# Two MLPs without their norm stage: x is transposed as it is, and the squared factor multiplies the MLP's sums

## The chip, the core and the metric

The kernel runs on one core of a Trainium2 chip. The metric is the device time of one execution, in microseconds (us). TensorE multiplies, VectorE and ScalarE evict and prepare, GpSimd (POOL) does little, and SyncE issues the loads of the weights. SBUF holds the data, and PSUM, in eight banks of 128 x 512 fp32, takes TensorE's results.

## The reference

Three blocks run on x (256 tokens by 1024). The change touches the two MLPs, one at the end of each of the first two layers:

```
def rmsnorm(x, g):
    xf = x.astype(jnp.float32)
    y = xf * lax.rsqrt(jnp.mean(xf * xf, axis=-1, keepdims=True) + EPS)
    return (y * g.astype(jnp.float32)).astype(x.dtype)

        x = x + jnp.concatenate([y_tok, y_mem], axis=-1) @ w_out[layer]
        hm = rmsnorm(x, mlp_norm[layer])
        x = x + jnp.square(jax.nn.relu(hm @ w_up[layer])) @ w_down[layer]
```

The factor r of a token, rsqrt(mean + EPS), is positive, and relu and the square let it through: square(relu(r a)) = r^2 square(relu(a)). So r^2 = 1 / (mean + EPS) may as well multiply the token's row of the MLP's result. The rest (a short convolution, attentions, RWKV, SSD, a router with 32 experts) is as before.

## The kernel before, in words

The program is a row of stages, each a block (`meeting`) at whose end all engines meet; only then does the next stage's work start. x lies in SBUF as two tiles of 128 tokens (`x[:, t, :]`). fp32 products are made in three parts: each operand is split into hi (rounded) and lo (the rest), and hi x hi, hi x lo and lo x hi are added up. ScalarE makes each hi part and VectorE each lo part from it.

Around an MLP stand three stages:

- **The output projection** (`add_projection`, a `split_stage` named out0 or out1). Two units of 1024 x 512 weights, each in two halves of four chunks (L449 to L468). The first half of a unit makes 24 products, the second 24. Jobs 0 and 1 are the two token tiles of x's first 512 columns, jobs 2 and 3 of its last 512; job j uses bank j. VectorE adds each full bank to x (L1203), in the order in which `programme` queues it: the split of piece 3 (L513), the additions of jobs 0 and 1, then `split_next` (L535), which splits the MLP's first unit early, then the additions of jobs 2 and 3. ScalarE has the hi parts of the same early split (L502).
- **The norm** (`norm`, L857). TensorE runs 11 warming products (L307). ScalarE and VectorE make the square sums of one token tile each (L871, L887), POOL the factor (L918, L920), both engines a scaled copy of x (L874, L892), TensorE 16 transposes (L910, L913) into eight banks, and ScalarE and VectorE evict each bank with the gain as hi (L879) and lo (L901) into `mlp_h`.
- **The MLP** (`mlp`, L1261). It first zeroes the four sums in banks 4 to 7 (L1304). A loop of four trips with two units each follows. Of a unit, the up products make four groups of 128 columns in banks 0 to 3. Each group takes eight steps k of two products, hi (L1315, 512 moving columns: hi and lo of h) and lo (L1313, L1318, 256). Sums are taken by ScalarE and VectorE two groups at a time: a copy (L1355), an addition (L1388), relu and square (L1391), hi (L1358) and lo (L1394) of the hidden part. 48 down products of three parts (L136 to L138) add into the four sums. Weights for the next unit are split meanwhile (L1349, L1381). At the end the sums are closed by a zero product each (L1255) and added to x (L1412).

Of the kernel before, what the change touches and what calls it, by code (L numbers as in the profile page):

```python
# [32 lines left out]
P = 128  # L33
S = 256
# [98 lines left out]
def three(pe, dst, left, right, start, stop):  # L133

    inside = not (start or stop)
    pe.matmul(dst, left[0], right[0], start=start, stop=False, skip_group_check=inside)  # L136
    pe.matmul(dst, left[0], right[1], start=False, stop=False, skip_group_check=inside)  # L137
    return pe.matmul(dst, left[1], right[0], start=False, stop=stop, skip_group_check=inside)  # L138


# [44 lines left out]
def program(nc, a, out, at, dumps=()):  # L185

    with ExitStack() as ctx:
# [167 lines left out]
        def split_stage(name, units, consume, src, pair=None, depth=3, on_vector=lambda j: j % 2 == 0, loads=(),  # L355
                        act_then=None, dve_then=None, on_pool=None, early=None, ahead=0, warm_after=0):

# [25 lines left out]
            with ExitStack() as on:  # L383
# [21 lines left out]

                def programme(split_w, split_h, empty, later=None, split_next=None):

# [23 lines left out]
                with meeting() as block:  # L431
# [6 lines left out]
                    def _(pe):  # L438
                        keep_warm(pe, 8)
                        for n, (u, first_chunk, products) in enumerate(units):  # L440
                            for half in range(2):
# [25 lines left out]
                                if half == 0 or not products[-1][6]:  # L467
                                    mm.then_inc(used, 1)  # L468
                        if warm_after:
                            quiet = max(0, n_full - n_banks)  # L470
                            pe.wait_ge(free_v if on_vector(quiet) else free_a, nth(quiet))
                            keep_warm(pe, warm_after, quiet % n_banks)

                    @block.scalar
                    def _(act):
# [27 lines left out]

                        programme(split_w, split_h, empty, split_next=split_next)

                    @block.vector
                    def _(dve):
# [28 lines left out]

                        programme(split_w, split_h, empty, later if dve_then else None, split_next)

# [654 lines left out]
        def mlp_first(layer, on):  # L1193

            u = unit[f"mlp{layer}"]
            w = [sb(f"mlp{layer}_w0_" + s, [P, 2, KD // 2, UC], F32R, on=on, side="right") for s in ("hi", "lo")]
            return w, lambda j: stream.view(u)[:, j * KD // 2:(j + 1) * KD // 2, :], u

        def add_projection(name, u0, src, early=None):
# [5 lines left out]
            split_stage(name, token_products(u0, 2), consume, src, on_vector=lambda j: True, depth=2, early=early)  # L1205

# [53 lines left out]

        def mlp(layer, h_both, w_first):  # L1261

# [14 lines left out]
            with ExitStack() as on:  # L1277
# [3 lines left out]
                hid = [sb("mlp_hid_" + part, [P, nm, S], F32R, on=on) for part in ("hi", "lo")]  # L1281
                rec = sb("mlp_rec", [P, nm, S], on=on)
                acc = lambda t, h: ps[:, 4 + 2 * t + h]

# [13 lines left out]
                with meeting() as block:  # L1298
                    @block.tensor
                    def _(pe):  # L1300
                        nought = c_("noughts").bitcast(BF16)
                        for t in range(NT):
                            for h in range(2):
                                pe.matmul(acc(t, h), nought[:, 0:P], nought[:, 0:UC], start=True, stop=False)  # L1304
                        with pe.Fori(0, trips) as i:
                            for b in range(body):
                                w = [[piece_slot(p, b * pieces + half) for p in w_split] for half in range(2)]
                                pe.wait_ge(w_lo, i * (body * pieces) + (b * pieces + 2))
                                for m in range(nm):
                                    for k in range(KD):  # L1310
                                        hi, lo = (p[:, k % 4, m * P:(m + 1) * P] for p in w[k // 4])
                                        if k:
                                            pe.matmul(ps[:, m, 0:S], lo, h_both[:, k, 0:S], start=False, stop=False,  # L1313
                                                      skip_group_check=True)
                                        mm = pe.matmul(ps[:, m], hi, h_both[:, k, :], start=(k == 0),  # L1315
                                                       stop=(k == KD - 1), skip_group_check=True)
                                        if not k:
                                            pe.matmul(ps[:, m, 0:S], lo, h_both[:, k, 0:S], start=False, stop=False,  # L1318
                                                      skip_group_check=True)
                                    if m % 2:  # L1320
                                        mm.then_inc(ups, 1)
                                for half in range(2):
                                    j = b * pieces + 2 + half
                                    w = [piece_slot(p, j) for p in w_split]
                                    pe.wait_ge(w_lo, i * (body * pieces) + (j + 1))

                                    pe.wait_ge(hid_lo, i * (body * nb) + (b * nb + half + 1))
                                    for k in range(2):
                                        f = 2 * half + k
                                        for t in range(NT):  # L1330
                                            for h in range(2):
                                                mm = three(pe, acc(t, h), [p[:, f, t * P:(t + 1) * P] for p in hid],
                                                           [p[:, k, h * UC:(h + 1) * UC] for p in w],
                                                           start=False, stop=False)
                                    mm.then_inc(downs, 1)
                        close_sums(pe, closed)

                    @block.scalar
                    def _(act):
# [25 lines left out]

                        act.activation(begun[:, 0:1], c_("noughts")[0:1, 0:1], ACT.Copy).then_inc(w_hi, 2)
                        for j in range(2, SPLIT):
                            split(0, j)
                        with act.Fori(0, trips - 1) as i:
                            for b in range(body):  # L1370
# [5 lines left out]
                    def _(dve):  # L1376
# [22 lines left out]

                        dve.tensor_copy(begun[:, 1:2], c_("noughts")[0:1, 0:1]).then_inc(w_lo, 2)  # L1400
                        for j in range(2, SPLIT):
                            split(0, j)
                        with dve.Fori(0, trips - 1) as i:
                            for b in range(body):
                                turn(i, b)
                        for b in range(body):
                            turn(trips - 1, b, last=b == body - 1)
                        for t in range(NT):
# [19 lines left out]
        def conv_layer(kn, first):  # L1428
            with ExitStack() as on:
# [72 lines left out]
                attention("mem_attn0", [memory_item(0, t, qT, nconv, [(1, 2, 4)]) for t in range(NT)], cat)  # L1502
                early = mlp_first(0, first)
                add_projection("out0", unit["out0"], cat, early)
                return early[0]

# [302 lines left out]
        def nsa_layer(sh, first, keys, held):  # L1809
            with ExitStack() as on:  # L1810
# [54 lines left out]
                inner.close()  # L1865
                early = mlp_first(1, first)
                add_projection("out1", unit["out1"], cat, early)
                return early[0]

# [1572 lines left out]

        def block_mlp(layer, w_first):
            with ExitStack() as on:
                h_both = sb("mlp_h", [P, KD, 2 * S], F32R, on=on)
# [95 lines left out]
```

## Time and profile before

| | us |
|---|---|
| median of 3 runs (1837.08 to 1841.11) | 1839.04 |
| span of the profiled execution | 1837.7 |
| TensorE busy in it | 1691.4 (92%) |
| VectorE busy | 921.0 (50%) |
| ScalarE busy | 601.6 (33%) |
| POOL busy | 34.3 (2%) |

Busy shares are means over stages with different limits. How long an engine's operations last says nothing of whether they are waited for; that is read in the timeline, from what stands idle before them and what released it. "PEq" as a releaser is a stage border or TensorE's queue. PEclk is the clock granted to TensorE: 1.00 is 2.4 GHz and 0.50 is 1.2 GHz. A product's record is longer than its distance to the next, since products are pipelined.

### The profile page before, as it was taken

How to read it: one execution, taken by the hardware profiler on the slowest of the kernel's cores; microseconds unless marked ns; L12 is line 12 of the kernel's file. 1: busy time of each engine (PE TensorE's matmuls, PEld its weight loads, DVE VectorE, ACT ScalarE, POOL GpSimd, SP SyncE). 2: the span in 40 equal slices, each digit the busy share in tenths (PEclk: the TensorE clock that was granted, in tenths of full speed). 3: DMA queues.
4: the chain of work that ended last, by engine and by line, in shares of the span. 5: the costliest groups of instructions: out<-in, count | busy, mean ns of one | idle time of the engine just before them, and what ended most of it. 6: DMA issues, size and time to landing. Idle time of an engine off the chain costs nothing. (4 is left out here: it accounts for less than half of the span.)

```text
span 1837.7 us, 31324 instructions
## 1 busy us (share of the span) xinstructions
PE 1691.4 (92%) x13407; PEld 1204.0 (66%) x13431; DVE 921.0 (50%) x1471; ACT 601.6 (33%) x875; POOL 34.3 (2%) x53
## 2 busy tenths in 40 slices
PE   7988999898789999998889999979979999999995
PEld 4976888665568887988887895557744444444442
DVE  2576555424865555787765775645642222121112
ACT  1534444213744444332003664534331111111110
POOL 2000000000000000010000000000000000000000
PEclk9999999998999999998999999989999999999998
DMA  8244454242074453420002541443579999999993
GB/s 316 93 183 183 183 183 160 92 147 92 7 269 183 183 183 114 168 88 14 4 4 93 184 145 63 160 166 110 205 301 429 427 426 428 427 427 427 427 427 150
DMA packets 101897, 379.91 MB, mean 207 GB/s; under 512 B 9980, under 2 KB 20463, under 8 KB 89227
## 3 DMA queue, kind: packets, MB, share of 16 engines
q1 hardware_dynamic: 101216, 377.89, 53.0%
q8 instruction: 98, 1.61, 0.4%
q14 instruction: 28, 0.23, 0.0%
q0 software_dynamic: 352, 0.15, 0.0%
q10 hardware_dynamic: 203, 0.04, 0.0%
HBM read 376.92 MB, written 1.14 MB: 206 GB/s over the span
## 5 line engine op out<-in xcount | busy, mean ns | idle before, releaser
L1315 PE MATMUL ps<-mlp_h,mlp_w_hi 128*128 128x512 f32 x512 | 179.1, 398 | 0.0
L3167 PE MATMUL ps<-weight_slots,moe_h 128*64 128x512 f32 x528 | 155.2, 594 | 6.8 <-DMA weight_slots<-in_w_exp_up 3.1
L1381 DVE TENSOR_TENSOR mlp_w_lo<-weight_slots,mlp_w_hi 128x2048 fp32r<-128x2048 f32 x60 | 134.9, 2290 | 45.6 <-ACT mlp_w_hi L1349 45.6
L3167 PE MATMUL ps<-moe_slots,moe_h 128*64 128x512 f32 x496 | 148.1, 593 | 4.0 <-DMA moe_slots<-in_w_exp_up 3.9
L3247 DVE TENSOR_TENSOR moe_hidT<-moe_silu,ps 128x256 f32<-128x256 f32 x32 | 13.5, 421 | 237.3 <-ACT moe_silu L3204 237.3
L1313 PE MATMUL ps<-mlp_h,mlp_w_lo 128*128 128x256 f32 x448 | 126.7, 283 | 0.0
L1349 ACT ACTIVATE mlp_w_hi<-weight_slots 128x2048 fp32r<-128x2048 f32 x60 | 111.4, 1904 | 43.0 <-PE ps L138 43.0
L3167 PEld LDWEIGHTS ps<-weight_slots,moe_h 128*64 128x64 f32 x528 | 50.4, 137 | 106.1 <-issue 105.3
L1315 PEld LDWEIGHTS ps<-mlp_h,mlp_w_hi 128*128 128x128 f32 x512 | 94.1, 190 | 17.5 <-issue 0.3
L136 PE MATMUL ps<-mlp_w_hi,mlp_hid_hi 128*128 128x512 f32 x256 | 101.3, 396 | 0.0
L138 PE MATMUL ps<-mlp_w_hi,mlp_hid_lo 128*128 128x512 f32 x256 | 101.2, 395 | 0.0
L137 PE MATMUL ps<-mlp_w_lo,mlp_hid_hi 128*128 128x512 f32 x256 | 101.2, 395 | 0.0
L307 PE MATMUL ps<-const 128*128 128x512 bf16 x309 | 77.7, 402 | 24.5 <-PEq L217 23.2
L1313 PEld LDWEIGHTS ps<-mlp_h,mlp_w_lo 128*128 128x128 f32 x448 | 85.9, 192 | 2.9
L3202 ACT ACTIVATE moe_grown<-ps 128x512 f32<-128x512 f32 x32 | 19.2, 599 | 209.4 <-PE ps L3167 209.4
L3167 PEld LDWEIGHTS ps<-moe_slots,moe_h 128*64 128x64 f32 x496 | 48.2, 137 | 49.2 <-issue 49.2
L3254 DVE SCALAR_TENSOR_TENSOR moe_y_lo<-ps,moe_slot_gate,moe_y_hi 128x512 fp32r<-128x512 f32 x32 | 24.0, 751 | 112.1 <-ACT moe_y_hi L3207 112.1
L3184 PE MATMUL ps<-moe_slots,moe_hidT 128*64 128x512 f32 x336 | 76.7, 598 | 1.0 <-DVE moe_hidT L3247 1.0
L307 PEld LDWEIGHTS ps<-const 128*128 128x128 bf16 x330 | 31.6, 102 | 63.9 <-issue 34.1
L3207 ACT ACTIVATE moe_y_hi<-ps,moe_slot_gate 128x512 fp32r<-128x512 f32 x32 | 22.0, 687 | 152.1 <-PE ps L3184 152.1
L2686 PE MATMUL ps<-weight_slots,hT 128*128 128x512 f32 x128 | 64.1, 624 | 0.0
L574 PE MATMUL ps<-weight_slots,hT 128*128 128x512 f32 (+2 forms) x160 | 58.6, 526 | 2.5 <-PEq L217 1.9
(641 smaller groups left out, 3944.9 us busy)
## 6 DMA issues: line engine op xcount, KB each, us to landing
weight_slots<-in_w_exp_gate SPq DMA_DIRECT2D x22, 2048.0 KB, 23.2
moe_slots<-in_w_exp_up SPq DMA_DIRECT2D x21, 2048.0 KB, 28.3
moe_slots<-in_w_exp_down SPq DMA_DIRECT2D x21, 2048.0 KB, 26.7
weight_slots<-in_w_in SPq DMA_DIRECT2D x20, 2048.0 KB, 7.9
weight_slots<-in_w_up SPq DMA_DIRECT2D x16, 2048.0 KB, 7.7
weight_slots<-in_w_down SPq DMA_DIRECT2D x16, 2048.0 KB, 7.6
weight_slots<-in_w_exp_up SPq DMA_DIRECT2D x11, 2048.0 KB, 27.2
weight_slots<-in_w_exp_down SPq DMA_DIRECT2D x11, 2048.0 KB, 25.7
```

The source lines that it names most:

```text
L136: pe.matmul(dst, left[0], right[0], start=start, stop=False, skip_group_check=inside)
L137: pe.matmul(dst, left[0], right[1], start=False, stop=False, skip_group_check=inside)
L138: return pe.matmul(dst, left[1], right[0], start=False, stop=stop, skip_group_check=inside)
L307: pe.matmul(ps[:, bank], nought[:, 0:P], nought[:, 0:UC], start=True, stop=True)
L574: mm = pe.matmul(dst, h[:, k, t * P:(t + 1) * P], w[:, k, c0:c0 + width], start=(first and k == 0), stop=(last and k == kc - 1))
L1313: pe.matmul(ps[:, m, 0:S], lo, h_both[:, k, 0:S], start=False, stop=False, skip_group_check=True)
L1315: mm = pe.matmul(ps[:, m], hi, h_both[:, k, :], start=(k == 0), stop=(k == KD - 1), skip_group_check=True)
L1349: act.activation(piece_slot(w_split[0], jj), raw_piece(jj), ACT.Copy).then_inc(w_hi, 1)
L1381: dve.tensor_tensor(piece_slot(w_split[1], jj), raw_piece(jj), piece_slot(w_split[0], jj).bitcast(F32), ALU.subtract).then_inc(w_lo, 1)
L2686: mm = pe.matmul(z_bank(g, t), hT[:, k, t * P:(t + 1) * P], w[:, k, :], start=(k == 0), stop=(k == KD - 1))
L3167: mm = pe.matmul(ps[side(kind), 0, :], h_sel[:, k, :], w[kind][:, k, :], start=(k == 0), stop=(k == KD - 1))
L3184: mm = pe.matmul(ps[side(h), 3, :], hid_T[:, f, :], w_down[:, f, h * UC:(h + 1) * UC], start=(f == 0), stop=(f == nm - 1))
```

## The change

There is no norm stage ahead of an MLP. x itself is transposed and multiplied by the gain alone. Its first 512 columns (`h_near`) are turned inside the last unit of the projection, between its halves: TensorE waits for x's first two additions and makes eight transposes into banks 4 to 7; ScalarE evicts hi and VectorE lo, both queued behind `split_next`. The last 512 columns (`h_far`) are turned at the start of the MLP stage. The up products of each unit now take two column groups together, near halves of both first, then far halves. The first trip is written out ahead of the loop, since in it TensorE waits for `h_far` and since its first down products open the sums, for which the zeroing products go. ScalarE makes the square sums in the MLP stage, behind its first two splits; VectorE makes the factor, and multiplies with it in the last additions.

```diff
+class Turning:
+    def tensor(self, pe, x_ready=None):
+        if x_ready is not None:
+            pe.wait_ge(x_ready, NT)
+        for c in range(KD // 2):
+            for t in range(NT):
+                mm = pe.transpose(self.bank(c)[:, t * P:(t + 1) * P], self.x(t, c), self.ident)
+            mm.then_inc(self.turned, 1)
+    def scalar(self, act):
+        for c in range(KD // 2):
+            act.wait_ge(self.turned, c + 1)
+            act.activation(self.part[:, c, 0:S], self.bank(c), ACT.Copy, scale=self.gain(c)).then_inc(self.led, 1)
+    def vector(self, dve):
+        for c in range(KD // 2):
+            dve.wait_ge(self.led, c + 1)
+            dve.scalar_tensor_tensor(self.part[:, c, S:], self.bank(c), self.gain(c),
+                                     self.part[:, c, 0:S].bitcast(F32), ALU.mult, ALU.subtract).then_inc(self.left, 1)
...
@@ split_stage: programme @@
                         if early and n == len(units) - 1:
                             split_next()
+                        if turn and n == len(units) - 1:
+                            turn()
                         for j in whole[0][n]:
                             empty(j)
@@ split_stage: tensor @@
+                                if turning and half == 0 and n == len(units) - 1:
+                                    turning.tensor(pe, free_v)
...
@@ mlp: tensor @@
-                        nought = c_("noughts").bitcast(BF16)
-                        for t in range(NT):
-                            for h in range(2):
-                                pe.matmul(acc(t, h), nought[:, 0:P], nought[:, 0:UC], start=True, stop=False)
-                        with pe.Fori(0, trips) as i:
+                        def unit_products(i, b, first=False):
...
+                            for m0 in range(0, nm, 2):
+                                for m, k in [(m0 + m, 4 * half + k) for half in range(2) for m in range(2)
+                                             for k in range(4)]:
+                                    if first and k == 4 and m == 0:
+                                        pe.wait_ge(turning.left, KD // 2)
...
+                                            mm = three(pe, acc(t, h), [p[:, f, t * P:(t + 1) * P] for p in hid],
+                                                       [p[:, k, h * UC:(h + 1) * UC] for p in w],
+                                                       start=first and f == 0, stop=False)
...
+                        turning.tensor(pe)
+                        for b in range(body):
+                            unit_products(0, b, first=b == 0)
+                        with pe.Fori(1, trips) as i:
                             for b in range(body):
+                                unit_products(i, b)
@@ mlp: scalar @@
+                        turning.scalar(act)
                         for j in range(2, SPLIT):
                             split(0, j)
+                        for t in range(NT):
+                            act.activation(squares[:, t, :], x[:, t, :], ACT.Square, scale=D ** -0.5,
+                                           accum_out=scale[:, 0, t:t + 1]).then_inc(summed, 1)
@@ mlp: vector @@
+                        turning.vector(dve)
                         for j in range(2, SPLIT):
                             split(0, j)
+                        dve.wait_ge(summed, NT)
+                        dve.tensor_scalar(scale[:, 0, :], scale[:, 0, :], EPS, None, ALU.add).then_inc(added, 1)
+                        dve.wait_ge(added, 1)
+                        dve.reciprocal(scale[:, 1, :], scale[:, 0, :]).then_inc(scale_made, 1)
...
-                                dve.tensor_tensor(part, part, acc(t, h), ALU.add)
+                                dve.scalar_tensor_tensor(part, acc(t, h), scale[:, 1, t:t + 1], part, ALU.mult, ALU.add)
@@ block_mlp @@
-                norm(f"mlp{layer}_norm", x, [("mlp_norm", layer * KD, [h_both[:, :, 0:S], h_both[:, :, S:]])])
-                mlp(layer, h_both, w_first)
+                mlp(layer, h_near, sb("mlp_h_far", [P, KD // 2, 2 * S], F32R, on=on), w_first)
```

## Rows read from the trace of the kernel before

**Rows 1.** Windows: from:to, length, busy us (instructions) by engine, PEclk, DMA share.

```profile
157.19:167.57 10.38, 5.33 (x31) 3.18 (x32) 6.17 (x14) 6.40 (x13) 0.95 (x2) 0.96 0.03 11
528.22:538.22 10.00, 4.96 (x31) 3.08 (x32) 6.17 (x14) 6.03 (x13) 0.94 (x2) 1.00 0.03 13
167.57:171.78 4.21, 4.21 (x19) 3.62 (x17) 3.25 (x2) 2.74 (x2) 0.00 (x0) 0.68 0.93 303
538.22:542.74 4.52, 4.52 (x18) 3.89 (x17) 3.18 (x2) 3.12 (x2) 0.00 (x0) 0.62 0.77 253
```

**Rows 2.** Timeline, projection's end to MLP: start, us, engine, line, operation, [idle, releaser].

```profile
156.80 0.39 PE L138 MATMUL ps<-out_w_hi,out_h_lo 128*128 128x512 f32 x1
157.23 0.69 DVE L1203 TENSOR_TENSOR x<-x,ps 128x512 f32<-128x512 f32 x1 [0.38 <-PE ps L138]
...
158.22 1.06 ACT L871 ACTIVATE mlp_norm_scaled<-x 128x1024 f32<-128x1024 f32 x1 [6.28 <-PEq L217]
...
158.45 2.32 PE L307 MATMUL ps<-const 128*128 128x512 bf16 x10 [1.26 <-PEq L217]
159.18 0.19 ACT L871 ACTIVATION_READ_ACCUMULATOR mlp_norm_scaled<-x 128x1 f32 x1
...
161.17 1.09 PE L910 MATMUL ps<-const,mlp_norm_scaled 128*128 128x128 f32 x8 [0.40 <-DVE mlp_norm_scaled L892]
...
162.10 1.04 PE L913 MATMUL ps<-const,mlp_norm_scaled 128*128 128x128 f32 x8
162.41 3.03 ACT L879 ACTIVATE mlp_h<-ps,cols 128x256 fp32r<-128x256 f32 x8 [0.63 <-PE ps L913]
162.99 3.23 DVE L901 SCALAR_TENSOR_TENSOR mlp_h<-ps,cols,mlp_h 128x256 fp32r<-128x256 f32 x8 [1.48 <-PE ps L913]
...
167.57 0.99 PE L1315 MATMUL ps<-mlp_h,mlp_w_hi 128*128 128x512 f32 x1
```

**Rows 3.** Groups by line, whole span: busy us, mean ns | idle before, releaser.

```profile
L136 PE MATMUL ps<-mlp_w_hi,mlp_hid_hi 128*128 128x512 f32 x256 | 101.3, 396 | 0.0
L138 PE MATMUL ps<-out_w_hi,out_h_lo 128*128 128x512 f32 x96 | 37.4, 390 | 0.0
L3254 DVE SCALAR_TENSOR_TENSOR moe_y_lo<-ps,moe_slot_gate,moe_y_hi 128x512 fp32r<-128x512 f32 x32 | 24.0, 751 | 112.1 <-ACT moe_y_hi L3207 112.1
```

**Rows 4.** Timeline of TensorE, first MLP's up products, over a change of bank.

```profile
171.55 0.63 PE L1315 MATMUL ps<-mlp_h,mlp_w_hi 128*128 128x512 f32 x2
...
172.25 0.39 PE L1315 MATMUL ps<-mlp_h,mlp_w_hi 128*128 128x512 f32 x1
```

**Rows 5.** Timeline, last unit of the first projection.

```profile
148.23 3.71 ACT L502 ACTIVATE mlp_w_hi<-weight_slots 128x2048 fp32r<-128x2048 f32 x2
...
150.57 1.28 DVE L1203 TENSOR_TENSOR x<-x,ps 128x512 f32<-128x512 f32 x2
...
151.59 0.39 PE L136 MATMUL ps<-out_w_hi,out_h_hi 128*128 128x512 f32 x1
...
151.76 4.49 DVE L535 TENSOR_TENSOR mlp_w_lo<-weight_slots,mlp_w_hi 128x2048 fp32r<-128x2048 f32 x2
```

**Rows 6.** Timeline of ScalarE and VectorE, first unit of the first MLP.

```profile
166.61 3.70 ACT L1349 ACTIVATE mlp_w_hi<-weight_slots 128x2048 fp32r<-128x2048 f32 x2
174.77 0.60 ACT L1355 ACTIVATE mlp_rec<-ps 128x512 f32<-128x512 f32 x1 [4.46 <-PE ps L1315]
...
177.52 0.70 DVE L1394 TENSOR_TENSOR mlp_hid_lo<-mlp_rec,mlp_hid_hi 128x512 fp32r<-128x512 f32 x1 [0.70 <-ACT mlp_hid_hi L1358]
```

**Rows 7.** Windows around the first MLP's end and the second norm; that norm's warming products.

```profile
347.80:351.30 3.50, 1.25 (x6) 0.44 (x7) 2.78 (x5) 0.32 (x1) 0.00 (x0) 0.98 0.00 0
351.30:355.30 4.00, 4.00 (x14) 1.68 (x13) 1.82 (x4) 1.98 (x3) 0.94 (x2) 0.59 0.02 4
534.20:537.50 3.30, 0.00 (x0) 0.00 (x0) 3.04 (x8) 2.25 (x7) 0.00 (x0) 1.00 0.00 0
...
529.48 2.32 PE L307 MATMUL ps<-const 128*128 128x512 bf16 x10 [1.26 <-PEq L217]
```

More of the change, by code:

```diff
@@ L138, in three, with __init__ @@
     return pe.matmul(dst, left[1], right[0], start=False, stop=stop, skip_group_check=inside)
+class Turning:
+    def __init__(self, x, bank, ident, part, gain, turned, led, left):
+        self.x, self.bank, self.ident, self.part, self.gain = x, bank, ident, part, gain
+        self.turned, self.led, self.left = turned, led, left
+    def tensor(self, pe, x_ready=None):
[14 more added lines that the diff above has]
+                                     self.part[:, c, 0:S].bitcast(F32), ALU.mult, ALU.subtract).then_inc(self.left, 1)
 class Stream:
@@ L355, in split_stage @@
         def split_stage(name, units, consume, src, pair=None, depth=3, on_vector=lambda j: j % 2 == 0, loads=(),
-                        act_then=None, dve_then=None, on_pool=None, early=None, ahead=0, warm_after=0):
+                        act_then=None, dve_then=None, on_pool=None, early=None, ahead=0, warm_after=0, turning=None):
             full, used, free_v, free_a = (sem(f"{name}_{s}") for s in ("full", "used", "free_v", "free_a"))
@@ L404, in after, with programme @@
                     return n + 3 if s.stop == half_chunks else s.stop
-                def programme(split_w, split_h, empty, later=None, split_next=None):
+                def programme(split_w, split_h, empty, later=None, split_next=None, turn=None):
                     for n in range(min(depth, n_pieces)):
@@ L502, in split_next @@
                                 act.activation(w[0][:, j], raw(j), ACT.Copy).then_inc(next_hi, 1)
-                        programme(split_w, split_h, empty, split_next=split_next)
+                        programme(split_w, split_h, empty, split_next=split_next,
+                                  turn=turning and (lambda: turning.scalar(act)))
                     @block.vector
@@ L535, in split_next @@
                                 dve.tensor_tensor(w[1][:, j], raw(j), w[0][:, j].bitcast(F32), ALU.subtract)
-                        programme(split_w, split_h, empty, later if dve_then else None, split_next)
+                        programme(split_w, split_h, empty, later if dve_then else None, split_next,
+                                  turning and (lambda: turning.vector(dve)))
                     @block.sync
@@ L1196, in mlp_first, with half_turning, add_projection @@
             w = [sb(f"mlp{layer}_w0_" + s, [P, 2, KD // 2, UC], F32R, on=on, side="right") for s in ("hi", "lo")]
-            return w, lambda j: stream.view(u)[:, j * KD // 2:(j + 1) * KD // 2, :], u
-        def add_projection(name, u0, src, early=None):
+            h_near = sb(f"mlp{layer}_h_near", [P, KD // 2, 2 * S], F32R, on=on, side="right")
+            return (w, lambda j: stream.view(u)[:, j * KD // 2:(j + 1) * KD // 2, :], u), h_near
+        def half_turning(name, layer, half, part, bank):
+            turned, led, left = (sem(f"{name}_{s}") for s in ("turned", "led", "left"))
+            c0 = half * KD // 2
+            return Turning(lambda t, c: x[:, t, (c0 + c) * P:(c0 + c + 1) * P], bank, ident, part,
+                           lambda c: col("mlp_norm", layer * KD + c0 + c), turned, led, left)
+        def add_projection(name, u0, src, early=None, layer=None, h_near=None):
             def consume(eng, j, bank, chain, vector):
@@ L1203, in consume @@
                 return eng.tensor_tensor(dst, dst, bank, ALU.add)
-            split_stage(name, token_products(u0, 2), consume, src, on_vector=lambda j: True, depth=2, early=early)
+            turning = h_near is not None and half_turning(name, layer, 0, h_near, lambda c: ps[:, 4 + c, 0:S])
+            split_stage(name, token_products(u0, 2), consume, src, on_vector=lambda j: True, depth=2, early=early,
+                        turning=turning)
         def turn_into(name, src, chunks, dst, dst0=0, scale=None):
@@ L1282, in mlp @@
                 rec = sb("mlp_rec", [P, nm, S], on=on)
+                squares = sb("mlp_squares", [P, NT, D], on=on)
+                scale = sb("mlp_scale", [P, 2, NT], on=on)
+                summed, added, scale_made = (sem(f"mlp{layer}_{s}") for s in ("square_sums", "added", "scale_made"))
+                turning = half_turning(f"mlp{layer}", layer, 1, h_far,
+                                       lambda c: ps[:, 4 + c, 0:S])
+                h_part = lambda k: (h_near, h_far)[k // 4][:, k % 4, :]
                 acc = lambda t, h: ps[:, 4 + 2 * t + h]
@@ L1300, in _ @@
                     def _(pe):
-                        nought = c_("noughts").bitcast(BF16)
-                        for t in range(NT):
-                            for h in range(2):
-                                pe.matmul(acc(t, h), nought[:, 0:P], nought[:, 0:UC], start=True, stop=False)
-                        with pe.Fori(0, trips) as i:
-                            for b in range(body):
[L1307 to L1335, printed above, removed]
@@ L1366, in _ @@
                         act.activation(begun[:, 0:1], c_("noughts")[0:1, 0:1], ACT.Copy).then_inc(w_hi, 2)
+                        turning.scalar(act)
                         for j in range(2, SPLIT):
                             split(0, j)
+                        for t in range(NT):
+                            act.activation(squares[:, t, :], x[:, t, :], ACT.Square, scale=D ** -0.5,
+                                           accum_out=scale[:, 0, t:t + 1]).then_inc(summed, 1)
                         with act.Fori(0, trips - 1) as i:
@@ L1502, in conv_layer @@
                 attention("mem_attn0", [memory_item(0, t, qT, nconv, [(1, 2, 4)]) for t in range(NT)], cat)
-                early = mlp_first(0, first)
-                add_projection("out0", unit["out0"], cat, early)
-                return early[0]
+                early, h_near = mlp_first(0, first)
+                add_projection("out0", unit["out0"], cat, early, 0, h_near)
+                return early[0], h_near
         def memory_queries(layer, q, qT):
@@ L1865, in nsa_layer @@
                 inner.close()
-                early = mlp_first(1, first)
-                add_projection("out1", unit["out1"], cat, early)
-                return early[0]
+                early, h_near = mlp_first(1, first)
+                add_projection("out1", unit["out1"], cat, early, 1, h_near)
+                return early[0], h_near
         def rwkv(by_a):
```

28 lines of the change are left out of this document (25 added, 3 removed).

## The prediction

> **What bounds it now.** I read the stretches around the two MLPs first, because the change touches nothing else. Between the last product of the projection before each MLP and the MLP's first product lie 10.38 and 10.00 us, in which TensorE issues only the norm's warming products, transposes and zeroing products [rows 1]. Then the timeline of the first of these stretches [rows 2] shows that each piece waits for the one before: the addition to x, the stage border, the square sums, VectorE's and ScalarE's scaled copy of x, 16 transposes, eight evictions in two halves (hi on ScalarE, lo on VectorE), another border, four zeroing products. So this gap is a chain and no engine's throughput; whatever leaves the chain is saved in full, as long as the MLP behind it is bound by TensorE. It is: its products have 0.0 us of idle time ahead of them [rows 3]. The first products behind each gap run slowly: the granted clock is 0.68 and 0.62 over the first eight double products, which take 4.21 and 4.52 us [rows 1]. In the same code at the full clock a step is 0.35 us (the products starting at 171.55 and 172.25 are two steps apart [rows 4]), so the eight would take 2.80.
>
> **The path after the change, for the first MLP.** The second MLP's stretch repeats the first, 371.03 us later (157.19 against 528.22 [rows 1]).
> - *In the projection stage.* TensorE finishes the first half of the last unit at 151.59, where the second half now starts. It must wait until VectorE has added the first two sums to x, at 150.57 + 1.28 = 151.85 [rows 5]; with the semaphore some 0.35 us lost. Then eight transposes: eight started within 162.10 - 161.17 = 0.93 us in the norm [rows 2]. With 0.07 for changing over, the second half starts 1.35 us later and TensorE ends that much later. Behind the waiting TensorE only this half is queued, and nobody but VectorE's last addition waits for its end.
> - *ScalarE* had its early splits from 148.23 and then nothing up to the norm [rows 2, 5]: its four hi parts (3.03 / 8 = 0.38 each [rows 2]) cost nothing; the cover is 6 us wide.
> - *VectorE* has the early splits until 151.76 + 4.49 = 156.25 [rows 5]. Four lo parts follow at 3.23 / 8 = 0.40 [rows 2], to 157.9, then the third addition, to 158.5. The last one needs TensorE's last product. It started at 157.23 and now starts at 157.23 + 1.35 = 158.58, ending at 159.27 in place of 157.92 [rows 2]. VectorE is thus covered, by 0.1 us only: were it later, the surplus would be on the path.
> - *Border and second half of the turning.* Between VectorE's last addition (to 157.92) and ScalarE's first work of the next stage (158.22) the border took 0.30 us [rows 2], and TensorE can start then as well. So the eight transposes start at 159.57; 0.93 plus 0.10 for changing over puts the first real product at 160.6 instead of 167.57. That is 6.97 us. For the second MLP it is 531.63 instead of 538.22, or 6.59.
> - *Products on the near half* need only what the projection stage left: eight steps, 2.8 us, to 163.4. Meanwhile ScalarE starts its first hi part 0.31 us after the second transpose of a chunk (162.10 to 162.41 [rows 2]), near 159.85. VectorE follows 0.58 later, needs 4 x 0.40, and is done near 162.1. The far half waits for nothing; slack 1.3 us.
> - *The clock.* The products run at full clock if it doesn't fall in the new, shorter gap: 4.21 - 2.80 = 1.41 and 4.52 - 2.80 = 1.72 us more.
> - *The MLP's helpers.* ScalarE ends the far half near 161.4, splits two pieces (3.70 us [rows 6]) to 165.1, and has the two square sums to make (1.06 us and 0.19 for the accumulator [rows 2], 2.4 together), to 167.5. The first two sums of the MLP are full at 160.6 + 16 x 0.35 = 166.2, so ScalarE takes them 1.3 us late. From that copy to the last of the hidden lo part the chain took 174.77 to 178.22, 3.45 us [rows 6]; it now ends near 171.0, with 0.1 for VectorE's two tiny factor operations. TensorE needs it after 32 steps, at 171.8. Hidden, with 0.8 us of slack; in later units ScalarE has its old time.
> - *The MLP's end.* Four additions become multiply-adds. A 128x512 addition from PSUM was 0.69 us [rows 2], a multiply-add of that shape and kind elsewhere 0.751 [rows 3]; 4 x 0.07 (rounded up) = 0.28 us lost per MLP. They lie on the path, since the border waits for them.
> - *At no cost:* the semaphore waits for the factor (made 170 us earlier), the weight DMAs that SyncE issues at the start of the MLP stage (some 7 us earlier, in front of data needed a unit later), POOL's two operations per norm, which go.
> - *The new order of products* (two column groups, near halves first, and only then the far halves) and the first trip written out ahead of the loop add no product. A change of PSUM bank costs nothing visible: the two steps from 171.55 to 172.25 hold one and take 0.70, as two plain ones do [rows 4]. I take 0, and bound it above by 0.02 us a change: the down products visit a bank for three products, the projection's for twelve, and a record is 0.396 against 0.390 us, 3 x 0.006 [rows 3]. 64 more changes in the MLPs' 16 units would then be 1.3 us. Below nothing: the whole 0.006 may come from where operands lie, and moves with the buffers.
>
> **The sum.** 6.97 + 6.59 + 1.41 + 1.72 - 2 x 0.28 = 16.1 us. The profiled execution's span is 1837.7 us, so the span becomes 1821.6. The median of the runs, 1839.04, lies 1.3 above that span; the forecast is **1823.0 us**. Everything behind the MLPs only moves forward, the expert weights' stream included, whose loads wait for buffers of the stages ahead of it.
>
> **Where the clock decides.** In the old kernel the clock fell after a break of over 3.3 us (nothing from 534.20 to 537.50 [rows 7], then 0.62 [rows 1]), and also at the MLP's end: TensorE works 1.25 of 3.50 us there, and the next 4 us have 0.59 [rows 7]. It did not fall over the 1.26 us break after the projection [rows 2]: the whole second gap has 1.00 [rows 1]. The new gap is about as short (158.55 to 159.57), if transposes count as work. They seem to: in the second norm the last plain product ended at 531.8, transposes followed, and from 534.20 to 537.50 the grant still was 1.00 with nothing running at all [rows 7].
> The Trainium skill (TensorE: Matmul & The Clock Gate, section Part 4: PE-mode transpose) says that transposes don't count as busy in the same way. By that rule the gap is 158.55 to 160.6, as long as the one at the MLP's end after which the clock fell, and both clock terms are lost. By the row above, transposes have kept the clock, so I give the rule the smaller chance.
>
> **Rivals.**
> 1. *The clock still falls* behind the new gap: 1.41 + 1.72 come back, 1826.1 us. For it: the gap and eight transposes together are 2.05 us. Against: the grant of 1.00 over 534.20 to 537.50. 12%.
> 2. *A helper chain becomes the wait*: VectorE is covered by 0.1 us at the border and ScalarE by 0.8 in the first unit. If either is 1 us later than reckoned in both MLPs, 1825 us; both, 1827. 8%.
> 3. *The change doesn't do what it says*, that is, the turning isn't taken beside other work: TensorE's wait for x falls behind VectorE's early splits (4.49 us), twice, 1832 us. Against: the additions of the first two sums come ahead of those splits in the timeline [rows 5]. 4%.
> 4. *The products themselves change* with the buffers' places: 0.396 to 0.390 is 1.5% [rows 3], of two MLPs of some 180 us (from 167.57 to about 347.8 [rows 1, 7]) 5 us less, 1818; or 1.3 us more. 8%.
> 5. *Slower*: each return to an unfinished sum's bank holds TensorE. Place: the up products, 64 more returns. At 0.02 us it costs 1.3 us. It decides from (16.1 + 3.7) / 64 = 0.31 us a return on, nearly a whole step; the time is then 1842.7 or more. Against: down products return to banks all the time with 0.0 idle [rows 3]. 3%.
> The Trainium skill (the same page, section on psum-queue depth-cycling) tells of a kernel whose clock swung because of such cycling through banks; no run here shows it.
>
> **Chances and range.** Forecast, within 2.5 us: 62%; rivals 12, 8, 4, 8 and 3%; 3% for what I haven't seen. Where the slow stretches fall depends on how each run meets the clock, at the MLPs' ends as well [rows 7]. The range 1817.5 to 1829.0 takes in rivals 1, 2 and 4 and leaves out 3, 5 and the rest, about 12%, and tails. A measurement here can tell 0.2% (3.7 us) from no change: faster by more than that 0.94, within it 0.03, slower 0.03.
>
> **What would show it.** No norm instructions between projection and MLP; eight transposes inside the last unit with VectorE's early splits behind them; 3.4 us from the projection's last product to the MLP's first; granted clock 1.00 over the first eight steps and those at 0.35 us; no wait at the far half or at the first down product; final additions near 0.75 us. Wrong would be a TensorE wait over 1 us at any of these places, or a step other than 0.35 in the loop.

## The result and the profile after

The changed kernel takes 1825.47 us (median of 4 runs, 1822.20 to 1826.99) against 1838.94 (1837.08 to 1841.11): ratio 0.9921, 95% interval 0.9906 to 0.9935, so 12.0 to 17.3 us less. The forecast was 1823.0 in a range of 1817.5 to 1829.0. The profiled execution's span is 1820.3 us, 17.4 below that of before.

The boundary, in the timeline of the changed kernel (start, us, engine, line, operation, [idle, releaser]); it answers [rows 2, 5]:

```profile
150.67 1.28 DVE L1245 TENSOR_TENSOR x<-x,ps 128x512 f32<-128x512 f32 x2
151.87 4.49 DVE L568 TENSOR_TENSOR mlp_w_lo<-weight_slots,mlp_w_hi 128x2048 fp32r<-128x2048 f32 x2
156.27 1.65 DVE L165 SCALAR_TENSOR_TENSOR mlp_h_near<-ps,cols,mlp_h_near 128x256 fp32r<-128x256 f32 x4
157.84 1.47 DVE L1245 TENSOR_TENSOR x<-x,ps 128x512 f32<-128x512 f32 x2
...
152.01 1.09 PE L154 MATMUL ps<-const,x 128*128 128x128 f32 x8
152.86 0.48 PE L136 MATMUL ps<-out_w_hi,out_h_hi 128*128 128x512 f32 x1
158.20 0.39 PE L138 MATMUL ps<-out_w_hi,out_h_lo 128*128 128x512 f32 x1
159.64 1.07 PE L154 MATMUL ps<-const,x 128*128 128x128 f32 x8 [1.04 <-PEq L245]
160.09 1.57 ACT L160 ACTIVATE mlp_h_far<-ps,cols 128x256 fp32r<-128x256 f32 x4 [0.27 <-PE ps L154]
160.46 0.48 PE L1363 MATMUL ps<-mlp_h_near,mlp_w_hi 128*128 128x512 f32 x1
```

The near half's transposes stand inside the projection's last unit, right behind x's first two additions. VectorE makes the near lo parts behind the early splits, and TensorE's last product (to 158.59) and VectorE's last addition (to 159.31) end within 0.7 us of each other. Between the projection's last product and the MLP's first, only the border and eight transposes are left. The windows show the clock (from:to, length, busy us of TensorE, its weight loads, VectorE, ScalarE, POOL, then the granted clock, DMA share, GB/s); they answer [rows 1, 7]:

```profile
158.59:160.46 1.87, 0.83 (x10) 0.85 (x9) 0.83 (x2) 0.58 (x3) 0.00 (x0) 1.00 0.00 0
160.46:163.35 2.89, 2.89 (x20) 2.53 (x18) 1.66 (x4) 2.89 (x6) 0.00 (x0) 1.00 0.76 203
340.80:343.40 2.60, 0.09 (x2) 0.08 (x2) 2.29 (x5) 0.07 (x1) 0.00 (x0) 1.00 0.00 0
343.40:347.40 4.00, 4.00 (x12) 1.67 (x13) 2.08 (x4) 2.23 (x3) 0.95 (x2) 0.60 0.00 0
```

The clock stays at 1.00 over the new gap and over the MLP's first eight steps, which take 2.9 us where they took 4.21 [rows 1]. At the MLP's end it falls as before. Between an MLP's first product and its last, TensorE has no wait in either MLP.

For comparing executions I cut each profile at two places: from the projection's first product to the start of the MLP's last addition to x. What lies between is the change's own stretch; everything else is code that the change doesn't touch. The columns, in us: projection (first product to last), gap (last product's start to the MLP's first), MLP (first product to last), tail (last product's start to the last addition's start), and their sum.

```
                        projection   gap      MLP      tail    stretch
before, first MLP          22.88    10.77   179.97    2.47    216.09
before, second MLP         22.90    10.39   180.29    2.47    216.05
changed, first MLP         24.17     2.25   179.11    2.73    208.27
changed, second MLP        24.19     2.25   179.11    2.74    208.30
```

So the change is worth 7.82 and 7.75 us, 15.6 in all. (The last multiply-add starts where this cut ends, and it is 0.06 us longer than the addition was: to the end of the last operation the two sums are 7.75 and 7.69 us, 15.4 in all.) The other 1.8 us by which the two profiles differ lie outside both stretches: 1405.5 us there before the change and 1403.7 after it. In the four profiles of the kernel before that part is 1404.4 to 1407.5 us, in the two of the changed kernel 1403.7 and 1406.0, so 1.8 us are within what the untouched stages vary by.

### The profile page after: what moved, and what is told of

Its sections match the earlier page's. It is cut to its first block and busy times, and to the rows that moved or that the text cites. A ratio compares the mean times of both kernels' runs of the same rounds, so it can differ in the third digit from the quotient of the medians.

```text
span 1820.3 us, 31222 instructions
## 1 busy us (share of the span) xinstructions
PE 1679.4 (92%) x13379; PEld 1195.5 (66%) x13401; DVE 917.1 (50%) x1467; ACT 600.6 (33%) x877; POOL 32.4 (2%) x49
## 5 line engine op out<-in xcount | busy, mean ns | idle before, releaser
L3311 DVE TENSOR_TENSOR moe_hidT<-moe_silu,ps 128x256 f32<-128x256 f32 x32 | 13.5, 421 | 237.9 <-ACT moe_silu L3268 237.9
L136 PE MATMUL ps<-mlp_w_hi,mlp_hid_hi 128*128 128x512 f32 x256 | 101.2, 395 | 0.0
L335 PE MATMUL ps<-const 128*128 128x512 bf16 x289 | 73.1, 404 | 22.6 <-PEq L245 21.3
L1363 PE MATMUL ps<-mlp_h_far,mlp_w_hi 128*128 128x512 f32 x256 | 90.9, 394 | 0.0
L1363 PE MATMUL ps<-mlp_h_near,mlp_w_hi 128*128 128x512 f32 x256 | 90.7, 397 | 0.0
L1361 PE MATMUL ps<-mlp_h_far,mlp_w_lo 128*128 128x256 f32 x256 | 71.7, 280 | 0.0
L136 PE MATMUL ps<-rwkv_in_h_hi,rwkv_in_w_hi 128*128 128x256 f32 x208 | 59.1, 284 | 0.6 <-DVE rwkv_in_w_lo L546 0.6
```

What stands on the lines that cost most here:

```text
L335: pe.matmul(ps[:, bank], nought[:, 0:P], nought[:, 0:UC], start=True, stop=True)
L1361: pe.matmul(ps[:, m, 0:S], lo, h_part(k)[:, 0:S], start=False, stop=False, skip_group_check=True)
L1363: mm = pe.matmul(ps[:, m], hi, h_part(k), start=(k == 0), stop=(k == KD - 1), skip_group_check=True)
```

## The experiments

**The changed kernel once more**

> The changed kernel once more, nothing edited. Theory: the change itself is worth 7.7 us at each MLP (between the projection's first product and the last addition of the MLP, 7.7 and 7.8 in the two profiles so far), 15.5 in all, and what lies above or below that in a run comes from where TensorE's slow stretches fall in stages the change doesn't touch. So the time is 1822 to 1827 and the stretch from the projection's first product to the MLP's last addition is again 208.3 us within 0.3, with a granted clock of 1.00 behind the border. Rival: the clock falls behind the new border in some executions; then that stretch is some 1.5 us longer and the clock over the first eight steps near 0.65.

It took 1825.20 us (1823.06 to 1826.26), ratio 0.9923 [0.9902, 0.9944] to 13 runs of the kernel before in the same job. Its stretches are 208.31 and 208.25 us, its clock 1.00 behind both borders. The rival was not seen: in none of the eight profiles of kernels without the norm stage (this section's others among them, sixteen borders) did the clock fall there.

**The order of the products taken back**

```diff
-                                for m, k in [(m0 + m, 4 * half + k) for half in range(2) for m in range(2)
-                                             for k in range(4)]:
+                                for m, k in ([(m0 + m, 4 * half + k) for half in range(2) for m in range(2)
+                                              for k in range(4)] if first else
+                                             [(m0 + m, k) for m in range(2) for k in range(KD)]):
```

> The changed kernel, but only the first unit takes near halves before far halves; every later unit finishes one column group before the next, as before the change. Theory: the 0.06 us by which each unit's up products are longer now (11.21 against 11.15) are the four more changes of bank, 0.015 each; they go, 0.42 us for seven units of an MLP, 0.85 in all. Rival: the new places of the buffers cost it; the up part of a unit stays at 11.21 us and nothing is gained.

1825.85 us, ratio 0.9927 [0.9908, 0.9947]. Neither figure came true, since the up part of a unit became longer. The timeline of the third unit in each kernel gives the up part as the distance from its first product to the first down product (L136): the kernel before, 224.85 - 213.70 = 11.15; the changed one, 216.57 - 205.36 = 11.21; this one 218.59 - 207.33 = 11.26:

```profile
213.70 0.39 PE L1315 MATMUL ps<-mlp_h,mlp_w_hi 128*128 128x512 f32 x1
224.85 0.40 PE L136 MATMUL ps<-mlp_w_hi,mlp_hid_hi 128*128 128x512 f32 x1
```

```profile
205.36 0.40 PE L1363 MATMUL ps<-mlp_h_near,mlp_w_hi 128*128 128x512 f32 x1
...
216.57 0.39 PE L136 MATMUL ps<-mlp_w_hi,mlp_hid_hi 128*128 128x512 f32 x1
```

```profile
207.33 0.39 PE L1364 MATMUL ps<-mlp_h_near,mlp_w_hi 128*128 128x512 f32 x1
...
218.59 0.39 PE L136 MATMUL ps<-mlp_w_hi,mlp_hid_hi 128*128 128x512 f32 x1
```

In these buffers the new order isn't what costs; it even saves 0.05 us a unit. What is left of the two theories is the rival's cause, the buffers' place; the experiment with one buffer, below, tests it.

**The norm kept, TensorE kept busy in it** (the kernel before, with one wait and 12 products more)

```diff
                             pe.transpose(ps[:, c, P:S], scaled[:, 1, c * P:(c + 1) * P], ident).then_inc(turned, 1)
+                        if in_parts:
+                            pe.wait_ge(left, 1)
+                            keep_warm(pe, 12, bank=0)
```

> The kernel before the change, norm stage and all, with 12 warming products in bank 0 behind the norm's transposes, as soon as VectorE has taken that bank. They fill TensorE's empty 3.3 us. Theory: 3.1 of the change's 15.5 us are the clock that no longer falls at the MLP's start; this kernel gains these alone, each MLP's first eight steps take 2.8 us instead of 4.2 to 4.5, and it runs some 2.5 to 3.5 us faster than the kernel before. Rival: warming doesn't hold the clock, or the clock's share of the gain is small: within 1 us of the kernel before.

The profile does what the theory says:

```profile
165.20:169.70 4.50, 3.81 (x20) 1.57 (x19) 3.37 (x9) 3.36 (x10) 0.00 (x0) 1.00 0.00 0
169.70:172.58 2.88, 2.88 (x18) 2.56 (x17) 1.54 (x1) 2.88 (x2) 0.00 (x0) 1.00 0.73 208
```

The clock is 1.00, and the stretches are 214.58 and 214.54 us, 1.51 each below the kernel before. Of the change's 7.8 us per MLP, 1.5 are the clock's. The times don't show it: 1838.40 us (median of nine; a tenth execution took 5067.19 us, for no reason that the record gives, and is left out), ratio 0.9997 [0.9983, 1.0011], at most 3.1 us gained, where 3.0 were in the stretches of the profile. In the profile itself the span is 1836.6 us, only 1.1 below that of before, and the part outside the stretches is 1407.4 us, near the upper end of the 1404.4 to 1407.5 of the kernel before. So the times fit the rival as well as they fit a gain of 3.0 us; what the clock at the MLP's start is worth is shown by the stretches alone.

**All of x turned in the MLP stage**

```diff
+                        near.tensor(pe)
                         turning.tensor(pe)
+                        pe.wait_ge(near.left, KD // 2)
```

(ScalarE and VectorE likewise make the near half ahead of the far one, and the projection's turning is off.)

> The changed kernel, but all eight chunks are turned at the start of the MLP stage, none in the projection. Theory: the projection ends 1.4 us earlier, as before the change; 16 transposes take 1.86 us and the first product also waits for the fourth lo part, near 2.9 us behind the stage's start, 161.2 us against 160.46: 0.7 us later per MLP; the far half is ready 1.6 us after that, so no wait there; but ScalarE and VectorE come 1.6 us later into the first unit, where the slack was 0.7 to 0.8 us, so some 0.8 us more is lost ahead of the first down product. In all 1.0 to 1.5 us slower per MLP, 2 to 3 us over the changed kernel, some 12.5 to 13.5 faster than the kernel before. Rival: turning beside the projection is what the change is worth; then most of the gain is lost.

1823.51 us, ratio 0.9912 [0.9892, 0.9932]. The stretches are 208.85 and 208.82 us: projection 22.90, gap 4.10, MLP 179.10. So turning half of x beside the projection is worth 0.55 us per MLP, since it gives back 1.3 of the 1.85 us that it takes out of the gap. The timed runs can't tell the two kernels apart: the medians even lie the other way, by 1.7 us. The rival falls, and so does my second loss of 0.8 us: ScalarE and VectorE came later, but so did the first product.

**One buffer for h at its old place** (the last kernel, with `mlp_h` as one buffer of eight chunks)

> The kernel that turns all of x in the MLP stage, with h in one buffer at the place it had before the change, in place of two buffers at two places. Order of products as in the changed kernel. Theory: where h lies costs the up products 0.06 to 0.11 us a unit (11.21 and, in the old order, 11.26, against 11.15 before); with one buffer the up part of a unit is 11.15 or a little less. Rival: the new order costs it and the place nothing; it stays at 11.21.

```profile
210.01 0.39 PE L1365 MATMUL ps<-mlp_h,mlp_w_hi 128*128 128x512 f32 x1
...
221.15 0.40 PE L136 MATMUL ps<-mlp_w_hi,mlp_hid_hi 128*128 128x512 f32 x1
```

11.14 us (and the MLP 178.60 where it was 179.10): the theory holds in the profile. Its one timed execution took 1826.37 us, which can't show half a microsecond. Order and turning are the same, and the up products' weights were allocated ahead of h and stay where they were. But h isn't all that moves: the buffers allocated behind it (the split weights of the down products, `mlp_hid`, `mlp_rec`), which other engines write meanwhile, move with its size. So the layout of the buffers is what costs; whether it is h's own place, its neighbours, or its being in two parts, no run shows.

**More transposes**

```diff
+                        for _ in range(3):
+                            for c in range(KD // 2):
+                                for t in range(NT):
+                                    pe.transpose(turning.bank(c)[:, t * P:(t + 1) * P], turning.x(t, c), ident)
                         turning.tensor(pe)
```

> The changed kernel with 24 more transposes of x ahead of the eight at the start of the MLP stage, so that TensorE does nothing but transposes for 3.7 us behind a border of 1.0 us. Theory: transposes count as work for the clock; it stays at 1.00 over the first eight steps, and the first product comes 24 x 0.116 = 2.8 us later than in the changed kernel, with nothing else lost. Rival, the page's rule that transposes don't count: TensorE then has been idle for 4.8 us, more than the 3.4 us that made the clock fall before the change, and the first eight steps run near 0.65 and take 1.4 to 1.7 us longer.

```profile
161.50:165.20 3.70, 3.40 (x31) 3.43 (x32) 0.14 (x1) 0.53 (x2) 0.00 (x0) 1.00 0.54 152
165.25:168.10 2.85, 2.85 (x19) 2.53 (x18) 1.66 (x4) 2.85 (x5) 0.00 (x0) 1.00 1.05 407
```

The first line's window holds the transposes: after 3.4 us of nothing else behind a break of 1.0 us the clock is 1.00, at both MLPs, and the gap grew by 2.63 us, a little less than the 2.8 expected. The execution took 1828.40 us. The Trainium skill (TensorE: Matmul & The Clock Gate, Part 4: PE-mode transpose) says that transposes don't count as busy in the same way, in a passage whose own measurement is of bf16. For these fp32 transposes this profile doesn't bear it out; the trace records them as MATMUL, so it doesn't tell whether they ran in the mode that the passage means.

**The last sums taken early** (the last trip written out; its last products finish the sums one by one)

```diff
+                                            if final and f == nm - 1:
+                                                mm.then_inc(closed, 1)
...
-                        with pe.Fori(1, trips) as i:
+                        with pe.Fori(1, trips - 1) as i:
                             for b in range(body):
                                 unit_products(i, b)
-                        close_sums(pe, closed)
+                        for b in range(body):
+                            unit_products(trips - 1, b, final=b == body - 1)
```

> The changed kernel with the MLP's last trip written out as well: each of the four sums is finished by its own last product, so VectorE's four last multiply-adds start one after the other while TensorE still works, and the four closing zero products go. Theory: from the MLP's last product to VectorE's last operation the tail shrinks from 2.73 to some 0.5 us, 2.2 us per MLP, 4.5 us in all; and the clock falls less often in the next stage, whose gap shrinks from 2.5 to some 1.3 us, up to 1 us more each. So 1819 to 1821 us. Rival: the multiply-adds are hidden, but the next stage waits for something else (POOL, a load), and less than 2 us are gained.

1817.85 us (1816.52 to 1821.00), ratio 0.9886 [0.9865, 0.9906]: the fastest kernel of this study, by the medians 7.4 to 7.6 us ahead of the changed one, whose runs were in other jobs. In the changed kernel VectorE starts its four multiply-adds 0.75 us behind the last product's start; here it is 1.59 ahead of it. First the changed kernel, then this one, whose last three lines are windows:

```profile
339.57 0.40 PE L138 MATMUL ps<-mlp_w_hi,mlp_hid_lo 128*128 128x512 f32 x1
340.03 0.81 PE L1299 MATMUL ps<-const 128*128 128x512 bf16 x3
340.32 2.73 DVE L1476 SCALAR_TENSOR_TENSOR x<-ps,mlp_scale,x 128x512 f32<-128x512 f32 x4 [8.08 <-remote]
```

```profile
341.46 2.77 DVE L1480 SCALAR_TENSOR_TENSOR x<-ps,mlp_scale,x 128x512 f32<-128x512 f32 x4 [5.74 <-PE ps L138]
343.05 0.40 PE L138 MATMUL ps<-mlp_w_hi,mlp_hid_lo 128*128 128x512 f32 x1
...
343.50:344.70 1.20, 0.00 (x0) 0.13 (x2) 0.89 (x3) 0.18 (x1) 0.00 (x0) 1.00 0.00 0
344.70:347.50 2.80, 2.35 (x11) 0.91 (x10) 1.65 (x4) 1.54 (x3) 0.94 (x2) 1.00 0.00 0
353.37:356.78 3.41, 3.41 (x9) 2.70 (x8) 0.00 (x0) 0.00 (x0) 0.00 (x0) 0.50 0.00 0
```

The stretches are 205.99 and 206.00 us, 2.3 less each. Of the 7.4 to 7.6 us that is 4.6; where the rest comes from isn't shown. The break behind the MLP is 1.3 us long now where it was 2.5, as forecast, and the clock doesn't fall within 5 us of either MLP's end. Behind the first MLP it falls all the same 10 us later (353.37). Nor is the shorter break shown to be the reason: with the turning all in the MLP stage, and with more transposes, the break is 2.5 us and the clock didn't fall at either MLP's end.

**ScalarE given more squares**

```diff
+                        for t in range(NT):
+                            act.activation(spare[:, t, :], x[:, t, :], ACT.Square, scale=D ** -0.5)
```

> The changed kernel with two more square passes over x on ScalarE (2.1 us) ahead of the two that count, their squares written as bf16. Theory: ScalarE's cover in the MLP's first unit is the distance from the hidden part's last lo (171.11 in the changed kernel) to the first down product (171.76), 0.65 us. So TensorE now waits 2.1 - 0.65 = 1.4 to 1.5 us ahead of its first down product, in each MLP, and the stretch from the projection to the last addition grows from 208.3 to 209.8 us. Rival: another wait (the weights' split, the square of the second pair) comes last there, and the wait is longer than 2 us, or the cover is wider and there is none.

```profile
172.71 0.61 ACT L1409 ACTIVATE mlp_rec<-ps 128x512 f32<-128x512 f32 x1
...
175.46 0.69 DVE L1454 TENSOR_TENSOR mlp_hid_lo<-mlp_rec,mlp_hid_hi 128x512 fp32r<-128x512 f32 x1 [0.70 <-ACT mlp_hid_hi L1412]
...
176.30 0.47 PE L136 MATMUL ps<-mlp_w_hi,mlp_hid_hi 128*128 128x512 f32 x1 [0.78 <-DVE mlp_hid_lo L1454]
```

The wait is where the theory had it, but the stretches grew by only 0.9 us each (209.24 and 209.22); the execution took 1824.34 us. Measured from the MLP's first product, ScalarE's copy came 1.9 us later, the hidden lo part 1.44. The 0.45 between them had been VectorE's: in the changed kernel its splits and factor held it until 168.31, while ScalarE's copy (167.22 to 167.82) lay ready. Another 0.5 was TensorE's distance: of the 0.65 us between the lo part and the first down product, 0.15 remain here, where TensorE does wait. I had read the slack from one engine's chain alone.

**The kernel before, three more profiles**

> The kernel before the change once more, nothing edited. Its profile had a slow stretch of TensorE's clock at the start of both MLPs, 1.5 us each of a stretch of 216.1 us from the projection's first product to the MLP's last addition; the kernel with a warmed norm lost these 3.0 us in its profile but not in its times. Theory: in other executions the clock doesn't fall there, or falls in one MLP only, so that the clock's part of the gain is smaller on the average than in the profile that was read. Then one or both stretches are near 214.6 us here with a clock of 1.00 over the first eight steps. Rival: both are 216.1 again, and the warmed norm lost its gain in other stages.

> The kernel before the change, nothing edited, for another profile. Its 22 timed executions lie in two heaps, near 1835.5 and near 1839 to 1843. Theory: they differ in where TensorE's slow stretches fall, at the MLP's starts among other places. If this execution is one of the lower heap, one or both MLP stretches are 214.6 us and not 216.1. Rival: the MLP stretches are 216.1 in a fast execution too, and the heaps come from other stages.

> As the run before this one, for one more profile of the kernel before the change. Theory: an MLP stretch of 214.6 us where the clock stays at 1.00 over the first eight steps, in a fast execution. Rival: 216.1 us in both MLPs in every execution.

They took 1841.57, 1839.35 and 1838.41 us. In all three, as in the first profile, the clock falls at the start of both MLPs, and the stretches are 216.0 to 216.1 us. None was one of the shortest executions (others, of which there is no profile, took 1834.9 to 1835.5), so whether those keep the clock at an MLP is open. In the four profiles at hand, eight MLPs, the 1.5 us are always lost.

## Why the prediction was right, step by step

- *The time beside the projection.* Forecast: half of the last unit starts 1.35 us later. Measured: the projection is 1.29 us longer (24.17 against 22.88). TensorE's wait for x and VectorE's order came as said.
- *VectorE at the border*, "covered, by 0.1 us only": its third and fourth additions run back to back (157.84, 1.47 us), the third ending at 158.52, the fourth starting at 158.63, 0.04 behind TensorE's end. The cover was the 0.1 that was forecast, and nothing was lost.
- *The first product*: forecast at 160.6, measured at 160.46, in an execution whose projection began 0.1 us later. Projection and gap together are 7.23 and 6.85 us shorter; the sum had 6.97 and 6.59. The eight transposes took 0.82 us up to the first product and not 1.03. The list at the prediction's end says 3.4 us from projection to MLP; this counted from the old end of the projection. By the working above it, it was 2.05 from the new end, and 1.87 were measured.
- *Far half*: ready at 160.59 + 1.66 = 162.25, needed at 163.35. No wait.
- *Helpers in the first unit*: the hidden lo part ends at 171.11 (forecast 171.0), the first down product comes at 171.76 (forecast 171.8).
- *The clock*, 1.41 + 1.72: it did not fall, and the warmed norm shows its price without the rest of the change: the MLP is 1.23 and 1.56 us shorter there (178.74 and 178.73 against 179.97 and 180.29). I had 0.18 and 0.16 too much, from counting every slow step against the steady 0.35 us: the first unit takes longer than later ones at full clock too (11.30 against 11.21 in the changed kernel, 11.34 against 11.15 with the warmed norm).
- *The products*, taken at 0 with a bound of 0.02 us per change of bank: this term was mis-sized, and its mechanism was wrong. The MLP is 179.11 us and not 178.74, 0.37 us lost in each. The change of bank isn't the cause, as the old order costs more in the new buffers (11.26); the layout of the buffers is (11.14 with one buffer), though not which part of it. That is rival 4's mechanism with its smaller price. Rival 5 never came near its 0.31 us a return.
- *The tail*: forecast 0.28 for four operations. Up to the fourth one's start it grew by 2.73 - 2.47 = 0.26, up to its end by 0.33. A multiply-add is 0.744 us.
- *The sum*: 16.1 forecast, 15.6 measured in the stretches. That it came so near is in part luck: over both MLPs the border gave 0.5 us more than forecast, the clock 0.3 and the products 0.7 less. Of the forecast's last step, the 1.3 us added to the span were the distance between a median and another execution; wherever a profiled run was itself timed, its time lies 1.8 to 2.0 us above its span. The medians differ by 13.5 and 12.9 us (both jobs). That the medians gained less than the profiles isn't explained: the executions of one kernel spread over 5 to 9 us (those of the kernel before from 1834.86 at a mean granted clock of 0.978 to 1843.53 at 0.971), and the interval (12.0 to 17.3) holds 15.6. It is a matter of the untouched stages, or of executions of the kernel before in which its clock didn't fall, which no profile caught.

## What to carry to other kernels

A stage that is one chain of short steps is worth its whole length when it goes, and most of that here came from not needing the norm's factor before the products, not from hiding work: 6.3 of 7.8 us are the chain, 1.5 the clock, and putting half of the turning beside the projection is only 0.55 of them. When two engines work in turn, read the slack of a wait from both queues; and look at the stage's other end, since four additions queued behind the MLP's last product cost another 2.3 us per MLP. Cut profiles at the change's own stretch before comparing, when the untouched rest varies by more than what is looked for.

## What was not expected of the hardware

- The same matmuls of the same data run at 11.14 to 11.26 us per unit, by the layout of the buffers in SBUF and the order in which the halves are taken. With h in one buffer at its old place the order hardly matters (11.15 and 11.14), in two buffers it does (11.26 and 11.21).
- The transposes kept the clock at 1.00 as ordinary products do, for at least 3.4 us. A break of 1.0 to 1.3 us didn't make it fall at any of these borders. At the MLP's end the break alone doesn't decide it. Without the norm stage it is 2.5 us there, and the clock fell within 5 us of the MLP's end at 9 of 14 ends; it stayed at both ends with all of x turned in the MLP stage, at both with more transposes, and at the first with more squares. With the norm stage it is 2.2 us, and the clock fell at all eight ends of the kernel before and at neither with the warmed norm.
